# A two-layer network and a mixing block on one Trainium2 core: gates of the recurrence between its projections, sigmoid written as tanh, the first norm's factor on the turning matmul, tiles on 64 bytes

## The reference

```python
hn = rms_norm(x, g0)                            # x * rsqrt(mean(x*x) + 1e-6) * g0
gate, xr = split(hn @ w_in, 2)                  # 1024 x 2048
gate = gelu(gate)
xc = conv_b + sum_k xpad[:, k:k+256] * conv_w[k]    # 4 causal taps per channel
r = sigmoid(blockdiag(xc, w_a) + b_a)           # 4 blocks of 256 x 256
i = sigmoid(blockdiag(xc, w_x) + b_x)
log_a = -8 * r * softplus(-lam);  a = exp(log_a)
u = sqrt(-expm1(2 * log_a)) * (i * xc)
h_t = a_t * h_(t-1) + u_t                       # scan over the 256 tokens
x = x + (h * gate) @ w_out
```

## Time and profile before

| | before |
|---|---|
| median of 3 runs | 927.99 us (927.28 to 929.76) |
| profiled execution, its own time | 928.35 us |
| its span | 926.5 us |
| TensorE busy | 901.2 us, 97% of the span |
| VectorE busy | 592.9 us, 64% |
| ScalarE busy | 472.7 us, 51% |
| GpSimd busy | 49.7 us, 5% |
| mean DMA rate | 178 GB/s |
| mean granted TensorE clock | 0.989 |

### The profile page before, as it was taken

The page is one execution under the profiler, slowest core; times in us unless marked ns, Lnnn a source line. Parts: engine busy times, 40 slices in busy tenths (PEclk is TensorE's granted clock), DMA queues, the critical chain, the costliest instruction groups (busy, mean ns, idle before and its releaser), DMA issues.

```text
span 926.5 us, 14824 instructions
## 1 busy us (share of the span) xinstructions
PE 901.2 (97%) x5970; PEld 797.9 (86%) x5970; DVE 592.9 (64%) x982; ACT 472.7 (51%) x769; POOL 49.7 (5%) x63
## 2 busy tenths in 40 slices
PE   7998999999999897999999999999999999999998
PEld 5997799999997895677989899987898889999996
DVE  6759675555554586826755655563567888888764
ACT  5587454444443556834545454453457675443550
POOL 0010000000000013300000000021110000000000
PEclk8999999999999998999999999999999999999999
DMA  8265785555545843408636545440424455544441
GB/s 328 100 227 179 273 307 192 189 192 188 183 138 182 318 138 125 148 1 326 245 134 250 185 180 187 176 163 31 163 77 159 160 205 174 191 155 164 158 161 46
DMA packets 28580, 164.46 MB, mean 178 GB/s; under 512 B 3168, under 2 KB 7648, under 8 KB 10080
## 3 DMA queue, kind: packets, MB, share of 16 engines
q1 hardware_dynamic: 28512, 163.51, 49.9%
HBM read 162.45 MB, written 1.05 MB: 176 GB/s over the span
## 4 chain that ended last, share of the span: by engine, by line
PE 91%; DVE 3%; ACT 2%; DMA 1%; issue 1%; POOL 1%; SPq 0%; POOLq 0%; DVEq 0%
PE ps L264 15%; PE ps L266 14%; PE ps L265 14%; PE ps L277 12%; PE ps L279 12%; PE ps L278 11%; PE ps L376 1%; PE ps L823 1%; PE ps L325 1%; PE ps L822 1%; PE ps L824 1%; DVE WL L1437 1%; PE ps L737 1%; PE ps L316 1%; PE ps L762 1%
## 5 line engine op out<-in xcount | busy, mean ns | idle before, releaser
L1437 DVE TENSOR_TENSOR WL<-RAW,WH 128x1024 fp32r<-128x1024 f32 (+1 forms) x264 | 310.7, 1215 | 118.6 <-ACT WH L899 117.9
L264 PE MATMUL ps<-XAh,WH 128*128 128x256 f32 x1152 | 330.3, 287 | 1.0 <-ACT XAh L935 0.6
L266 PE MATMUL ps<-XAh,WL 128*128 128x256 f32 x1152 | 327.4, 284 | 0.0
L265 PE MATMUL ps<-XAl,WH 128*128 128x256 f32 x1152 | 327.3, 284 | 0.0
L899 ACT CAST WH<-RAW 128x1024 fp32r<-128x1024 f32 (+1 forms) x264 | 261.4, 1041 | 70.7 <-PE ps L279 65.8
L264 PEld LDWEIGHTS ps<-XAh,WH 128*128 128x128 f32 x1152 | 222.1, 193 | 10.0 <-issue 7.6
L265 PEld LDWEIGHTS ps<-XAl,WH 128*128 128x128 f32 x1152 | 222.1, 193 | 1.4 <-issue 0.2
L266 PEld LDWEIGHTS ps<-XAh,WL 128*128 128x128 f32 x1152 | 222.1, 193 | 0.0
L278 PE MATMUL ps<-WL,HTh 128*128 128x512 f32 x256 | 101.5, 396 | 0.0
L279 PE MATMUL ps<-WH,HTl 128*128 128x512 f32 x256 | 101.4, 396 | 0.0
L277 PE MATMUL ps<-WH,HTh 128*128 128x512 f32 x256 | 101.4, 396 | 0.0
(11 more groups left out here) (245 smaller groups left out, 1133.9 us busy)
## 6 DMA issues: line engine op xcount, KB each, us to landing
RAW<-in_w_dram SPq DMA_DIRECT2D x144, 1024.0 KB, 5.0
GB<-in_gb_dram SPq DMA_DIRECT2D x5, 512.0 KB, 5.9
BI<-in_dbias_dram SPq DMA_DIRECT2D x16, 128.0 KB, 2.1
NB<-in_nbias_dram SPq DMA_DIRECT2D x16, 128.0 KB, 2.2
RAW<-in_w_dram SPq DMA_DIRECT2D x2, 528.0 KB, 3.5
X<-in_x_dram SPq DMA_DIRECT2D x4, 256.0 KB, 3.7
CX<-in_ctx_dram SPq DMA_DIRECT2D x2, 512.0 KB, 5.0
out_dram<-X SPq DMA_DIRECT2D x3, 256.0 KB, 2.1
```

The lines of the kernel that those rows point to most:

```text
L264: T.e.matmul(dst, h, xh[:, k, :], start=k == 0, stop=False)
L265: T.e.matmul(dst, h, xl[:, k, :], start=False, stop=False)
L266: last = T.e.matmul(dst, l, xh[:, k, :], start=False, stop=k == 7)
L1437: D.e.tensor_tensor(M.WL[:, c.s, sl], M.RAW[:, c.r, sl], M.WH[:, c.s, sl].bitcast(F32), ALU.subtract).then_inc(*S.lo.tick(key, a))
```

## The change

- TensorE, ScalarE and VectorE take the recurrence block by block: the gate matmuls of block 0 stand between xr 2 and xr 3, those of 1 and 2 behind xr 3, those of 3 behind gate 0.
- sigmoid(z) becomes (1 + tanh(z/2)) / 2; the halves go into scales and biases (NC4, PC4, HB), a 0.25 into the scale of the sqrt. Exp and tanh stand side by side for each block. a*a moves from VectorE to GpSimd, i * xc from GpSimd to VectorE.
- The two `ri` pieces get a tile of their own, RI, on the place of XB, and leave RAW and its order.
- The first norm's gain comes as one row of 4 KB and is spread over the partitions by two matmuls with a row of ones; x is multiplied with it before 1/rms is known. 1/rms goes on the diagonal of a 128 x 128 matrix (GpSimd), and the turning becomes a plain float32 matmul with that matrix, in banks 6, 7 and, for the second half, 2, 3.
- Piece xr 0 comes in two DMAs. The identity comes behind all of x.
- `tile` rounds to 64 bytes.

The diff, cut to its core:

```diff
-    p += [(("xr", j), ("B", "rec_w_in", 0, 1024 + 256 * j)) for j in range(4)]
-    p += [(("ri", half), ("R", "rec", 0, half)) for half in range(2)]
+    p += xr[:3] + ri[:1] + xr[3:] + ri[1:]
...
+        at = self.top
         self.XB = self.tile("XBh", [128, 8, 256], F32R), self.tile("XBl", [128, 8, 256], F32R)
+        self.top = at
+        self.RI = self.tile("RI", [128, 2, 2048])
...
-        at, self.top = self.top, self.top + (n + 31) // 32 * 32
+        at, self.top = self.top, self.top + (n + 63) // 64 * 64
...
+def first_transposes(T, M, S, t):
+    T.wait_ge(*S.diag.at(t))
+    for n in range(2):
+        b = turn_bank(0, t, n)
+        T.wait_ge(*S.xn.at(0, t, n))
+        for q in range(4):
+            at = n * 512 + q * 128
+            made = T.e.matmul(M.PS[b][:, q * 128:(q + 1) * 128], M.XN[:, t, at:at + 128], M.RI[:, 1, t * 128:(t + 1) * 128], start=True, stop=True)
+        made.then_inc(*S.tr.tick(0, t, n))
...
+    T.wait_ge(*S.zeros.at("on"))
+    T.wait_ge(S.grow, 16)
+    for n in range(2):
+        T.e.matmul(M.PS[n][:, :], M.AR[0:1, 1, 0:128], M.GB[0:1, 0, n * 512:(n + 1) * 512], start=True, stop=True).then_inc(*S.gain.tick(n))
...
+    recurrent(0)
+    recurrent(1)
+    recurrent(2)
+    recurrence_gates(0)
+    recurrent(3)
+    recurrence_gates(1)
+    recurrence_gates(2)
+    gate(0)
+    recurrence_gates(3)
+    gate(1)
+    gate(2)
+    gate(3)
...
+    def decays(blk):
+        A.wait_ge(*S.lam.at("hb"))
+        for which in range(2):
+            b = (2 * blk + which + 4) % 8
+            dst = (M.RT, M.IT)[which]
             A.wait_ge(*S.ri.at(blk, which))
             for m in range(2):
-                A.e.activation(dst[:, blk, m * 256:(m + 1) * 256], M.PS[b][:, m * 256:(m + 1) * 256], AF.Sigmoid,
-                               bias=M.cc(bias, 2 * blk + m)).then_inc(*S.sig.tick(blk, which, m))
+                half_bias = M.lam2("HB")[:, 8 * which + 2 * blk + m:8 * which + 2 * blk + m + 1]
+                A.e.activation(dst[:, blk, m * 256:(m + 1) * 256], M.PS[b][:, m * 256:(m + 1) * 256], AF.Tanh,
+                               scale=0.5, bias=half_bias).then_inc(*S.sig.tick(blk, which, m))
+        A.wait_ge(*S.lam.at("pc4"))
+        for name, dst, func in (("NC4", M.AT, AF.Exp), ("PC4", M.SN, AF.Tanh)):
+            for m in range(2):
+                A.wait_ge(*S.sig.at(blk, 0, m))
+                c4 = M.lam(name)[:, 2 * blk + m:2 * blk + m + 1]
+                A.e.activation(dst[:, blk, m * 256:(m + 1) * 256], M.RT[:, blk, m * 256:(m + 1) * 256], func,
+                               scale=c4, bias=c4).then_inc(*S.decay.tick(blk, name, m))
+    first_tap(0)
+    high(A, M, S, "xr", 3)
+    first_tap(1)
+    high(A, M, S, "gate", 0)
+    first_tap(2)
+    decays(0)
+    first_tap(3)
+    decays(1)
+    high(A, M, S, "gate", 1)
+    decays(2)
+    high(A, M, S, "gate", 2)
+    decays(3)
     high(A, M, S, "gate", 3)
...
+    gained(0, 0)
     variance(D, M, S, 0, 0)
+    gained(0, 1)
+    gained(1, 0)
     variance(D, M, S, 0, 1)
-    norm_scaled(D, M, S, 0, 0)
-    norm_scaled(D, M, S, 0, 1)
+    gained(1, 1)
...
+    taps(0)
+    softplus_series(D, M, S)
+    low(D, M, S, "xr", 3)
+    taps(1)
+    low(D, M, S, "gate", 0)
+    taps(2)
+    taps(3)
+    drive(0)
+    low(D, M, S, "gate", 1)
+    drive(1)
+    low(D, M, S, "gate", 2)
+    drive(2)
+    drive(3)
     low(D, M, S, "gate", 3)
...
+    for blk in range(4):
         for m in range(2):
-            P.wait_ge(*S.sig.at(j, 1, m))
-            P.wait_ge(*S.conv.at(2 * j + m, 3))
-        P.e.tensor_tensor(M.IT[:, j, :], M.IT[:, j, :], two(M.XC, j), ALU.mult).then_inc(*S.ix.tick(j))
+            P.wait_ge(*S.decay.at(blk, "NC4", m))
+            P.wait_ge(*S.decay.at(blk, "PC4", m))
+        P.e.tensor_tensor(M.RT[:, blk, :], M.AT[:, blk, :], M.AT[:, blk, :], ALU.mult).then_inc(*S.asq.tick(blk))
...
-    gain(0)
-    for key in M.ORDER[:3]:
-        chunk(key)
+    Y.e.dma_start(M.GB[0:1, 0, :], D["gb"][0, 0:1, :]).then_inc(S.grow, 16)
+    tokens(0)
+    tokens(1)
+    Y.e.dma_start(M.CP[:, 0:128], D["cp"][:, 0:128]).then_inc(S.ident, 16)
...
+    chunk(("xr", 1))
+    chunk(("xr", 2))
+    recurrence(0)
     Y.e.dma_start(M.CP[:, 128:C["end"]], D["cp"][:, 128:C["end"]]).then_inc(S.rest, 16)
+    chunk(("xr", 3))
+    recurrence(1)
     gain(1)
```

More of the change, by code:

```diff
@@ L215, in __init__ @@
         self.CH = chunks()
-        self.ORDER = [key for key, _ in order()]
+        self.ORDER = [key for key, _ in order() if self.CH[key].i is not None]
         self.SPLIT = [key for key in self.ORDER if self.CH[key].m is not None]
@@ L254, in columns_matmul @@
     c, (xh, xl) = M.CH[key], x
-    for m in range(2):
+    for m, a in ((0, 0), (0, 1), (1, 0), (1, 1)):
         dst = M.PS[bank][:, m * 256:(m + 1) * 256]
[L257 to L266, removed]
+        T.wait_ge(*S.hi.at(key, a))
+        T.wait_ge(*S.lo.at(key, a))
+        if xready is not None:
+            xready(a)
+        for k in range(4 * a, 4 * a + 4):
+            h, l = weights_of(M, c, k * 256 + m * 128, 128)
+            T.e.matmul(dst, h, xh[:, k, :], start=k == 0, stop=False)
+            T.e.matmul(dst, h, xl[:, k, :], start=False, stop=False)
+            last = T.e.matmul(dst, l, xh[:, k, :], start=False, stop=k == 7)
     return last
@@ L304, in rows_last_two, with turn_bank @@
                     made.then_inc(*S.acc.tick(stage, t, n))
+def turn_bank(k, t, n):
+    return 2 + n if k == 0 and t else 6 + n
 def norm_transposes(T, M, S, k, t):
@@ L941, in scalar_rec @@
     norm_high(A, M, S, 0, 0)
-    high(A, M, S, "xr", 0, halves=(0,))
+    A.wait_ge(S.first, 16)
+    high(A, M, S, "xr", 0, halves=(0,), whole=False)
     norm_high(A, M, S, 0, 1)
@@ L1552, in vector_rec, with taps @@
     conditioning(D, M, S)
-    low(D, M, S, "xr", 3)
-    for j in range(4):
+    def taps(j):
         for k in range(1, 4):
@@ L1592, in gated_low @@
         D.e.tensor_tensor(M.XB[1][:, sl, :], M.XC[:, sl, :], M.XB[0][:, sl, :].bitcast(F32), ALU.subtract).then_inc(*S.ybl.tick(j))
-    scan(0)
-    scan(1)
-    for j in range(4):
-        gated(j)
-        low(D, M, S, "wout", j, halves=(0,))
-        if j < 2:
-            scan(j + 2)
-        gated_low(j)
-        low(D, M, S, "wout", j, halves=(1,))
+    for j in range(2):
+        forced(j)
+    for j in range(2):
+        scan(j)
+    gated(0)
+    low(D, M, S, "wout", 0, halves=(0,))
+    gated_low(0)
+    low(D, M, S, "wout", 0, halves=(1,))
+    gated(1)
+    forced(2)
+    gated_low(1)
+    low(D, M, S, "wout", 1)
+    scan(2)
+    forced(3)
+    scan(3)
+    gated(2)
+    low(D, M, S, "wout", 2)
+    gated_low(2)
+    gated(3)
+    gated_low(3)
+    low(D, M, S, "wout", 3)
 def scales(D, M, S):
@@ L2362, in signals @@
     S.ident, S.rest, S.uk, S.uv, S.out = (landed(n) for n in ("ident", "rest", "uk", "uv", "out"))
+    S.grow, S.first, S.ri_in = landed("grow"), landed("first"), [landed(f"ri{i}") for i in range(2)]
     split = [(key, a) for key in M.SPLIT for a in range(2)]
@@ L2372, in signals @@
     S.tr, S.warm = count("tr", norms), count("warm", one)
+    S.gain = then(S.warm, range(2))
     S.ri = count("ri", [(blk, which) for blk in blocks for which in range(2)])
@@ L2397, in signals @@
     halves = [(blk, m) for blk in blocks for m in range(2)]
-    S.tanh = count("decays", halves)
-    S.decay = then(S.tanh, halves)
+    S.decay = count("decays", [(blk, name, m) for blk in blocks for name in ("NC4", "PC4") for m in range(2)])
     S.sqrt = then(S.decay, blocks)
@@ L2433, in signals @@
     S.conv = count("conv", [(ch, k) for j in blocks for k in range(1, 4) for ch in (2 * j, 2 * j + 1)])
-    S.asq = count("drives", blocks)
-    S.drive = then(S.asq, blocks)
-    S.forced = then(S.drive, blocks)
-    S.scan = count("scan", halves)
+    S.drive, S.forced = count("drives", blocks), count("forced", blocks)
+    S.ix, S.scan = count("ix", blocks), count("scan", halves)
     S.y, S.ybl, S.otl = (count(n, blocks) for n in ("y", "ybl", "otl"))
```

150 lines of the change are left out of this document (84 added, 66 removed).

## The result

On one chip, in turn with the kernel before, the changed kernel takes 923.34 us (median of 6 runs, 920.88 to 925.84) against 929.19 (6 runs, 927.28 to 930.70). The ratio is 0.9944, with an interval of 0.9922 to 0.9966. So the change gains 5.85 us where the forecast had 10.4 (918 against the profiled execution's 928.35; its sum has 10.5). 923.34 lies inside the range, but 5.3 above the predicted 918. The kernel before has 929.19 here, over 6 runs, and had 927.99 over the three that were known. The profiled execution of the changed kernel is one of its longest, 925.58 us (span 923.8), so its trace shows only 2.7 us less than that of before (span 926.5).

What follows compares the result with a forecast made beforehand. TensorE was taken to bound the kernel, busy for 901.2 of 926.5 us. From the profiled execution, 928.35 - 6.05 (tiles) - 4.45 (gap before wout) - 0 (start) = 917.85, stated as 918; range 914.5 to 925.5.

Steps and rivals of the forecast that it cites:

- Tiles: HT and MT matmuls: stationary tiles on 64 bytes save 7 ns on each of 864, 6.05 us; bounds 0 and 7.8.
- The forecast's own sign, 227 ns from start to start: Down-projection and last-projection matmuls at 227 ns would prove the tile step right, 234 wrong.
- the 5 us beyond wout: Prediction wrong if the span beyond wout is not 5 us or more shorter, or if wout ends later than 101.
- Rival B: HT and MT matmuls: the 32 bytes are not the cause, so 6.05 us are not gained, 924; chance 0.17.
- The gap before wout: Recurrence: the 3.25 us gap and 1.90 of slow clock go, a 0.7 wait for wout 3 comes; 4.45 gained.
- Rival C: Recurrence: VectorE's chain 3 us later, wout 3 waits 3.7 and a slow stretch of 1.9 follows, 923; chance 0.12.
- The start: First norm and turning: xr 0 begins at about 15.8; 0.6 gained or 0.6 lost by the clock, taken as 0.
- rival E: Start: gains' row lands after 8 us or slow clock lasts; 2 to 3 us lost, 920.5; chance 0.01 alone.
- Rival D: ScalarE: ten table loads between tanh and exp, 12.8 us, plus slow clock; up to 16.6 lost, 934.6; chance 0.03.

Runs made afterwards that it cites:

- phase128: The changed kernel with HT 128 bytes and MT 384 bytes further on; 919.82 us against 929.34 for the kernel before, ratio 0.9896.
- recurrence_alone: The kernel before with only the recurrence's new order, tanh for sigmoid and RI, without tile step or new start; 924.42 us, ratio 0.9951 to before.
- combined: The changed kernel with phase128's tile places, spreading matmuls over 128 rows and wout 3's split ahead of the last product's steps; 918.21 us, ratio 0.9861 to before.
- all_shifted: The changed kernel with every tile 128 bytes further on; 925.47 us, ratio 0.9933 to the kernel before.
- old_start: The changed kernel with the start of the kernel before; 924.94 us, ratio 0.9951 to the kernel before.
- sigmoid_back: The changed kernel with Sigmoid in place of Tanh for r and i, which adds two table loads a block; 931.92 us, ratio 1.001 to the kernel before.
- fill_one_row: The changed kernel with three more one-row matmuls behind the spreading ones, their output unread; 923.24 us, ratio 0.9932 to the kernel before.
- fill_all_rows: The changed kernel with spreading and three unread fill matmuls over 128 rows, gain tile cleared first, row sent behind x; 921.54 us, ratio 0.9922 to before.

## Why the prediction was wrong, step by step

**Tiles: the step that failed.** The prediction put it so: "After the edit HT and MT lie on 64 [...] at 7 ns each that is 864 x 0.007 = 6.05 us". The 7 ns were read rightly from the earlier trace rows, and that the place of the stationary tile causes them was right too (phase128 returns 4.2 us in the trace). Wrong was the measure, the step from "32 bytes off" to "on 64 it costs nothing". XB and WH differ by a multiple of 256 bytes, and this, not lying on 64, made 227 ns; the edit moved HT from a distance of 96 to one of 128, for 1.8 ns x 864 = 1.6 us, and in time 0.2 was measured. Put in the sum, 918 + 6.05 - 1.6 = 922.4, against 923.34 measured; and with 929.19 for the kernel before, 929.19 - 10.5 + 4.45 = 923.1. The forecast's own sign, 227 ns from start to start, didn't come (232), and neither did the 5 us beyond wout: the span from wout's end on is 1.2 us shorter, and wout ended at 102.04, not before 101. The prediction's two facts (XB on 64, HT 32 off) fitted any measure under which the two differ. Working out each tile's address modulo 128, 256 and 512 before choosing would have shown that "64" was one guess of several. Rival B gave 924 for "the offset isn't the cause", 0.7 from the time measured; its reason is half right, since place was the cause and the 32 bytes were not. The sentence from the Trainium skill, page "SBUF — State Buffer", section Specifications (16-byte lines), gave 0 for the edit. That is nearer to the 0.2 measured than my 6.05, but every distance tried is a multiple of 16, and they differ by up to 9 ns, so that rule doesn't explain the rows either.

**The gap before wout: right.** Forecast -4.45; the trace has -3.85 and recurrence_alone -4.6. The -4.6 is a median and the -3.85 a trace, and they agree within the interval of recurrence_alone. The wait of 3.25 and the slow clock behind it went, and wout 3 became late, as forecast: I had 89.6 for its low part and 88.9 for TensorE's need, a wait of 0.7, and measured are 92.17 and a wait of 1.0. Both are some 2.5 later than forecast, and wout had begun 2.2 late (78.89 against 76.7). Tanh and exp do share a table. A pair of exp or tanh on RT shows 1.09 us, not 0.92, but pairs overlap: the three on the chain take 0.84 + 0.98 + 0.99 = 2.81 us, where I had 3 x 0.92 = 2.76. That there is one more wait is confirmed by combined, which takes it away. Before any block's gates there is no TensorE wait. Rival C (923) comes nearest to the measured time, by luck: its wait of 3.7 for wout 3 was 1.0, and no slow clock stood behind it.

**The start: not settled in time.** Forecast 0 with bounds of 0.6, xr 0 at 15.8. In the profiled execution xr 0 began at 18.21: warming ended 0.5 us later than before, and the clock was slow over nearly all of the turning, 6.58 us where I had allowed 3.6 to 5.3. In the profile of all_shifted, with the same start, it began at 15.93, so the schedule was right there and its spread from run to run was left out. I had named this in rival E (both halves slow, 2 to 3 us lost) and gave it 0.01, as if the fall could only come where it came in the earlier trace rows. In 4 of the 5 experiments that keep one-row spreading, a fall came again, for 6.8 us in phase128 and 3.4 in the three others, and xr 0 started between 15.93 and 18.47. Over the medians, old_start shows no loss.

**Rival D: right in kind, wrong in size, and absent here.** After has one load before 66 us, at 0.73, where before had three. When eight loads are forced in, sigmoid_back loses 8.6 us in the median and 4.6 in the trace; I had 16.6 for ten.

Together: forecast -10.5. From it 4.45 are missing by the tile step. Of the 5.85 measured, recurrence_alone has 4.6. The 1.2 left is of the size of the 1.6 that the tile rows show, and within the error of each; what the start adds or takes isn't resolved. The last line of the sum also slipped: 917.85 less 0.4 is 917.5, not 918.

## What to carry to other kernels

A difference between two tiles supports a cause only when every property in which they differ has been listed: for a place in memory, the addresses of both operands of the instruction, and their distance under several moduli. Where float32r matmuls of 512 columns set the time, try the stationary tile and the tile that streams past it at the same address modulo 256; here that was a shift of 128 bytes (384 for MT) and 4.2 us in the trace. Other widths and types were not tried. A helper's chain that is shortened is worth the wait that it ended, minus the wait of what came behind it, so look at once for that next one.

## What the runs showed of the hardware that I had not expected

- A float32r matmul of 512 columns starts every 227 ns if the two operands' distance is 0 modulo 256 bytes, and every 231 to 236 otherwise (32 to 192 tried in steps of 32). With every tile moved by 128 bytes nothing changed, and the 5 ns are there too while all other engines and the DMAs stand still (232.1 against 226.6). These are means: behind a wait even a distance of 0 runs slower for a while (after, XB from 93.08 to 94.47: 232 ns).
- The clock was granted at half for 3.4 or 6.8 us behind matmuls of one row, without any pause of TensorE ahead of it (fill_one_row), and not behind the same with 128 rows (fill_all_rows): 5 of 6 profiles against 0 of 4. It is supported, not settled, and it fell in 4 of 4 profiles with the start of before, which has no such matmuls.
- The time of one kernel comes in groups 2.3 us apart (921.0, 923.3, 925.7) that follow the mean granted clock (0.998, 0.993, 0.991). Why an execution falls into one of them is open.
